# Differential mixer's end: squares ahead of the weight roundings, two gate groups inside the output norm, modulation units one place forward

## What is computed

```python
def diff_attention(...):                      # DA
    def attend(q, k, v):
        s = jnp.einsum('bhmqd,bhmkd->bhmqk', q, k).astype(jnp.float32) * scale
        a = jax.nn.softmax(s, axis=-1)
        a = a[:, :, 0] - lam * a[:, :, 1]
        return jnp.einsum('bhqk,bhkd->bhqd', a.astype(v.dtype), v)
    def finish(o):
        return merge_heads(rmsnorm(o, sub_gain) * (1.0 - lam_init))
...
def hgrn2_mixer(...):                         # HG
    for f, lb in ((f_fw, lower_bound[0]), (f_bw, lower_bound[1])):
        f = lb + (1.0 - lb) * jax.nn.sigmoid(f.astype(jnp.float32))
        dirs.append((split_heads(jnp.log(f), HG_HEADS, HG_DK), split_heads(1.0 - f, HG_HEADS, HG_DK)))
...
for layer in range(DEPTH):
    mod_l = [m[:, None, :] for m in adaln_params(c, w_mod[layer], b_mod[layer])]
    p_l = split_cols(modulate(x, norm1_g[layer], mod_l[0], mod_l[1]) @ w_in[layer])
```

## Time and profile before

| what | value |
|---|---|
| median of three runs | 2334.16 us |
| profiled execution | 2332.5 us |
| its span | 2330.7 us |
| TensorE matmul busy | 2095.5 us (90%) |
| VectorE busy | 999.5 us (43%) |
| ScalarE busy | 784.6 us (34%) |
| GpSimd busy | 697.1 us (30%) |
| mean granted TensorE clock | 0.941 of full speed |

### The profile page before, as it was taken

How to read it: one execution, slowest core, us unless ns; L and a number is a source line. 1 busy time by engine, 2 the same in 40 slices (tenths; PEclk the granted TensorE clock), 3 DMA queues, 4 the chain that set the end, 5 groups by cost and what they waited for, 6 DMA issues and landing times.

```text
span 2330.7 us, 31996 instructions
## 1 busy us (share of the span) xinstructions
PE 2095.5 (90%) x13292; PEld 1752.7 (75%) x13292; DVE 999.5 (43%) x1771; ACT 784.6 (34%) x1281; POOL 697.1 (30%) x573
## 2 busy tenths in 40 slices
PE   5799898878978899999999988998978788999998
PEld 3678786757767788888888866777767667778787
DVE  2545547845674541222213253445847644221222
ACT  1533323423443531222213153223435445232231
POOL 0231211011732323223232222223014433444542
PEclk9899998989988999999999998998989879999999
DMA  8220010451321111212212123010242311322222
GB/s 281 48 71 19 21 35 19 163 140 39 109 73 55 55 55 55 73 55 63 65 55 72 55 45 74 19 37 23 88 109 79 109 55 59 104 91 91 91 91 73
DMA packets 179216, 169.72 MB, mean 73 GB/s; under 512 B 29232, under 2 KB 176128, under 8 KB 178944
## 3 DMA queue, kind: packets, MB, share of 16 engines
q1 hardware_dynamic: 176704, 161.12, 22.6%
q10 hardware_dynamic: 2368, 6.55, 0.9%
HBM read 159.79 MB, written 2.10 MB: 69 GB/s over the span
## 4 chain that ended last, share of the span: by engine, by line
PE 76%; DVE 9%; ACT 7%; issue 3%; DMA 2%; SPq 2%; POOL 1%; DVEq 0%; ACTq 0%; POOLq 0%
PE gp L841 56%; PE sp L1047 3%; PE gp L1084 2%; PE sp L1193 2%; PE tp L1064 1%; SPq L692 1%; PE gp L869 1%; POOL HGx_kd L744 1%; PE sp L1038 1%; DVE small L2073 1%; ACT nt L1372 1%; PE sp L888 1%; PE sp L948 1%; PE op L1064 1%; PE op L1084 1%
## 5 line engine op out<-in xcount | busy, mean ns | idle before, releaser
L756 POOL TENSOR_TENSOR wlo<-raw,whi 128x512 fp32r<-128x512 f32 x392 | 524.6, 1370 | 1348.2 <-ACT whi L1339 1266.8
L841 PE MATMUL gp<-xhi,whi 128*128 128x512 f32 (+1 forms) x1486 | 542.2, 365 | 36.1 <-DVE xlo L1875 21.4
L841 PE MATMUL gp<-xhi,wlo 128*128 128x512 f32 (+1 forms) x1486 | 528.5, 356 | 0.0
L841 PE MATMUL gp<-xlo,whi 128*128 128x512 f32 (+1 forms) x1408 | 502.9, 357 | 0.0
L841 PEld LDWEIGHTS gp<-xhi,whi 128*128 128x128 f32 x1486 | 288.9, 194 | 86.2 <-issue 11.3
L1339 ACT ACTIVATE whi<-raw 128x2048 fp32r<-128x2048 f32 x98 | 186.9, 1908 | 454.2 <-PE gp L841 424.2
L841 PEld LDWEIGHTS gp<-xhi,wlo 128*128 128x128 f32 x1486 | 287.9, 194 | 41.0
L841 PEld LDWEIGHTS gp<-xlo,whi 128*128 128x128 f32 x1408 | 273.7, 194 | 38.6 <-issue 2.0
L841 PE MATMUL gp<-hhi,whi 128*128 128x512 f32 (+1 forms) x768 | 276.5, 360 | 9.6 <-issue 5.0
L841 PE MATMUL gp<-hlo,whi 128*128 128x512 f32 (+1 forms) x768 | 274.9, 358 | 0.0
L841 PE MATMUL gp<-hhi,wlo 128*128 128x512 f32 (+1 forms) x768 | 274.7, 358 | 0.0
(11 more groups left out here) (349 smaller groups left out, 3210.0 us busy)
## 6 DMA issues: line engine op xcount, KB each, us to landing
raw<-in_w_ff SPq DMA_DIRECT2D x64, 1024.0 KB, 5.4
raw<-in_w_mod SPq DMA_DIRECT2D x48, 1024.0 KB, 5.2
raw<-in_w_in SPq DMA_DIRECT2D x20, 1024.0 KB, 5.4
raw<-in_w_in SPq DMA_DIRECT2D x24, 256.0 KB, 4.4
raw<-in_w_out SPq DMA_DIRECT2D x8, 768.0 KB, 4.7
bias<-e SPq DMA_DIRECT2D x96, 32.0 KB
xin<-in_x ACTq DMA_DIRECT2D x1, 2048.0 KB, 9.6
raw<-in_w_out SPq DMA_DIRECT2D x16, 128.0 KB, 4.8
```

Source lines behind the costliest of these rows:

```text
L756: nc.gpsimd.tensor_tensor(wlo[:, s % 2, ks, :], raw[:, index[splits[s]] % 2, ks, :], whi[:, s % 2, ks, :].bitcast(F32), ALU.subtract).then ...
L841: mm = pe.matmul(out, lhs, rhs, start=(i == 0 and j == 0), stop=(i == KT - 1 and j == 2))
```

## The change

Three things change. In `fill_plan` each modulation unit is listed one chunk earlier. TensorE's `out_norm` of DA computes the first two groups of HGf0 itself: the first between the sums and the transposes, the second behind the transposes; `hgrn` then starts HGf0 at its third group. ScalarE stops filling from step 21 on in layer 0 (13 in layer 1), takes the squares, and only then goes through the last five slots, so that both gate roundings stand behind the squares.

```diff
@@ -166,7 +166,7 @@
                 closing = i + 1 < len(chunks) and chunks[i + 1][0] != u
-                while not closing and put < len(units) * (i + 1) // len(chunks):
+                while not closing and put < min(len(units) * (i + 2) // len(chunks), len(units)):
                     work.append((units[put], "row", 3))
...
                 if m == "DA":
-                    out_norm("DA", l, buf("DA", "y"))
-
-            def out_norm(m, l, y):
+                    u = ("prj", l, "HGf0")
+                    out_norm("DA", l, buf("DA", "y"), [lambda i=i: dense(u, chunks_of(u)[i]) for i in range(2)])
+
+            def out_norm(m, l, y, beside=None):
...
                     mm.then_inc(ls(l, m + "_oms"), 1)
+                if beside:
+                    beside[0]()
...
                     mm.then_inc(ls(l, m + "_orstd"), 1)
+                if beside:
+                    beside[1]()
...
                     u = ("prj", l, name)
-                    for c in chunks_of(u):
+                    for c in chunks_of(u)[2 if name == "HGf0" else 0:]:
                         dense(u, c)
...
-                    if n >= 1:
+                    if n >= 1 and (m != "DA" or n <= len(units) - 4):
                         fill(ENDS[m, l][n - 1])
                 if m == "DA":
-                    fill(ENDS[m, l][-2])
-                    fill(ENDS[m, l][-1])
                     end = LAT if l == DEPTH - 1 else T
                     act.wait_ge(*upto(l, "DA_oread", pairs_of("DA", l)))
                     for i in range(2):
                         nc.scalar.activation(buf("DA", "y")[:, i, 0:end], mix[:, i, 0:end], ACT.Square)\
                           .then_inc(ls(l, "DA_osq"), 1)
+                    for slot in ENDS[m, l][-5:]:
+                        fill(slot)
                     out_norm("DA", l, buf("DA", "y"))
```

## The result

The changed kernel takes 2343.01 us, the median of six runs (2340.62 to 2346.88). The kernel before, on the same chip, took 2334.77 (2330.51 to 2336.15, six runs). The ratio is 1.003 with a 95% interval of 1.0016 to 1.0043: the change made the kernel slower by 0.3%. The forecast was 2335 with 2327 to 2342. The measured 2343.01 lies 1.0 above that range; by the ratio, on the 2334.16 that the forecast was worked from, it is 2341.2, just inside. Either way it is 6 to 8 us above the 2335, and of the three cases the slower rival (2342.4) is the one that came.

What follows compares the result with a forecast made beforehand. The prediction took TensorE, with 76% of the chain of waits, to bound the kernel. Terms +5.3 +2.1 +1.75 -5.5 -2.3 = +1.35 on 2332.5 gave 2333.9, plus 1.66 for the median 2335.5, rounded to 2335; range 2327 to 2342.

Steps and rivals of the forecast that it cites:

- the slower rival: Low clock behind most new light steps of DA, four of five in layer 1; sum +8.2, 2342.4 us; chance 0.25.
- the +5.3: Layer 1, steps 6 to 15: chunks moved into odd steps with `weigh`, alternating 4.64 and 6.8; 56.1 against 50.8 us.
- The second sum for the heavy step: Layer 1's heavy odd step checked from step 3: 5.98 plus 0.8 for an eighth of a chunk and a turn, 6.8 us.
- The terms -5.5 and -2.3: End of DA, layers 0 and 1: HGf0 ends at T+33.0 instead of T+38.5, and T+31.0 instead of T+33.3.
- at two in seven and 1.5 us: DA's light steps: two of seven such places bring a low-clock stretch behind them, each costing 1.5 us.
- the clock in the slots: Low-clock cost behind light DA steps, five places in layer 1 and seven in layer 0: +2.1 and +3.0 us.
- the groups of steps of the prediction: Layer 0's DA steps 2 to 23 in four groups at full clock: 38.5, 12.8, 39.5, 15.1, in all 105.9 us.
- the forecast's +1.35: Sum of all terms, DA's steps and ends in both layers, against the profiled 2332.5 us.
- The rival's point of decision (six stretches): Low-clock stretches in DA's steps from which the slower case holds: 3.4 us more than the forecast's 3.4 stretches (5.1 us).
- the norm wins: No low clock in DA's output norm (-8.9 and -5.7) or the new light steps; -7.6, 2326.6 us; chance 0.25.
- the two cancel: The forecast case: the output norm's gain is spent in DA's slots; between 2329.5 and 2338.8 us; chance 0.5.

Runs made afterwards that it cites:

- e9: Kernel before with layer 1's slot 6 left empty and all later contents one slot later, order of work unchanged; 2351.31 us, ratio 1.0058.
- e1: Kernel before with the new plan alone (modulation units listed one chunk earlier); 2336.83 us against 2337.64, ratio 1.0001.
- e2: Changed kernel with the old plan, so only the squares and HGf0 group edits; 2334.42 us, ratio 0.9986 to the kernel before.
- e3: Kernel before with only the squares put ahead of the roundings, no HGf0 groups in the norm; 2327.57 us, ratio 0.9954.
- e6: Changed kernel with HGf0's four groups put back behind the transposes; 2337.59 us, ratio 0.9996 to the kernel before.
- e5: Changed kernel plus ten unread matmuls in DA's light even steps to keep TensorE busy; 2342.12 us, ratio 1.0016 to the kernel before.
- e10: e4 with the new plan line (modulation units one chunk earlier); 2340.28 us, ratio 1.001 to the kernel before.
- e8: e7 plus ten unread matmuls in light even steps; 2324.73 us, ratio 0.994 to the kernel before.
- e4: As e3, with the output norm's factors and spreading also ahead of the deferred roundings; 2323.91 us, ratio 0.9944 to the kernel before.
- e7: As e4, but only the last three slots deferred instead of five; 2322.03 us, ratio 0.9936 to the kernel before.

## Why the prediction was right in the steps and wrong in the clock

**Right: the structure of the steps.** Layer 1 alternates between 4.6 and 6.8 wherever the clock is full, which was the +5.3. With the three low stretches taken off (1.5 each, from 8.32 against 6.79) its 60.78 is 56.2; 56.1 was forecast. (The second sum for the heavy step was loose: an eighth of a chunk and a turn are 0.37 and 0.34, so 6.7 and not 6.8. The first gave 6.85, and 6.79 came.) e9 confirms the reason: it is the exchange between the two kinds of step.

**Right: the end of DA.** Squares at T+0.0, transposes held by HGf0's first group at T+12.6 and T+11.4, TensorE idle for 6.32 and 5.22 before the third group, HGf0's last matmul done at T+33.5 and T+30.9 against T+33.0 and T+31.0 forecast. The terms -5.5 and -2.3 came out as -5.4 and -2.3. The path was right event by event. Where the gain comes from was not: the working gives it to the wait and the roundings that the edit on ScalarE takes away, and allows the plan only one load that comes a step earlier. But the plan's later T alone gives -5.4 and -9.1 (e1), and the other two edits alone -2.9 and -0.7 (e2). The terms hold for the three edits together and for none of them by itself. Nor was the use of the groups questioned: they cost 6 us (e2, e3) to 9 us (changed kernel, e6), and the -5.5 was what was left of a larger gain of the squares.

**Wrong: "at two in seven and 1.5 us".** The term of the sum that failed is the clock in the slots, forecast as +2.1 and +3.0 for 3.4 low stretches of 1.5 us. There were seven: in layer 0 those of steps 7, 12 with 13, 15, and 19, in layer 1 those of steps 9, 13 and 15. In layer 1 they cost 4.6 (60.78 less the 56.1 without them), which is the forecast's price of 1.5 each. In layer 0 the price was wrong too. Each of its slow steps ran at full clock in another kernel with the same plan: 5.49 (e5) instead of 8.59 in step 7, 4.45 and 7.77 (e10) instead of 5.40 and 10.40 in 12 and 13, 6.41 (e10) instead of 7.96 in 15, 4.24 (e5) instead of 6.96 in 19, 3.83 (e1) instead of 4.12 in 20. With these, the groups of steps of the prediction come out as follows:

| steps | forecast, full clock | measured | measured, less the low clock |
|---|---|---|---|
| 2 to 9 | 38.5 | 41.8 | 38.7 |
| 10 to 12 | 12.8 | 13.5 | 12.5 |
| 13 to 19 | 39.5 | 46.0 | 39.1 |
| 20 to 23 | 15.1 | 15.1 | 14.8 |

Together 116.4, and 105.1 without the low clock, against 105.9: the structure of layer 0 was forecast to within 1 us, and four stretches of low clock cost 11.2 us, 2.8 each instead of 1.5. So the low clock cost about 15.8 us in both layers instead of 5.1. These 10.7 us more, less the 0.8 by which layer 0's structure came out shorter, are the way from the forecast's +1.35 to the measured +11.5. The rival's point of decision (six stretches) was passed. That its sum of +8.2 equals the timed +8.2 (2343.01 less 2334.77) is in part luck: it takes eight stretches at 1.5, 12 us of low clock, and the stretches of the trace add up to +11.5. The frequency was taken from seven places of a kernel in which such steps stand alone; the change sets them in a row, each before a heavy step without slack, and there three or four of the five heavy steps 7 to 15 of layer 1 ran at a low clock (e1, e6, e9, e10 and the changed kernel).

For layer 1 the cause is shown, not only argued. With TensorE busy for 4.40 us in the light steps instead of 3.20, all heavy steps behind them run at 1.00 (e5). With the order of the units as before but light and heavy steps alternating, the low clock comes too (e9). Layer 0 fits: the low stretches behind step 2 all began in or behind a step with idle time to which no matmuls had been added, in e5 and e8 as well. This agrees with the Trainium skill, "TensorE: Matmul & The Clock Gate", section "A second HAM failure mode: psum-queue depth-cycling", which tells of a kernel in which short idle times between groups of matmuls make the clock swing and cost throughput: here idle times of 1.4 us in 4.6 suffice, in most places. The prediction had the rule, as a rival at 0.25. Two low stretches out of seven were read as a rate that carries over to any place; it is not a rate.

**The other two rivals.** That the norm wins did not happen: a low clock came in both norms (the sums took 3.80, and the 48 matmuls behind the idle stretch 10.18). That the two cancel is what e1 shows of the plan with the old end, by another way than forecast: not the norm gave it back, but the loads.

**What stays open.**
- What makes the clock fall behind one light step and not behind another. In e9 the steps 1676.98 and 1689.90 are alike but for the last digits (3.19 busy of 4.63, clock 1.00 in both), and 8.29 follows one and 6.79 the other. Where the idle time falls within the step was not varied. Why the low clock lasted two and three times as long in steps 7, 12 with 13, and 19 of layer 0 is open too.
- Why e1 times as before though its stretches of DA are 5.9 longer in sum. Step 5 of layer 1, which lies ahead of the stretches and holds the same work in all kernels, shows how much the clock outside the stretches can shift: 5.34 in before and in the changed kernel, 6.45 to 6.47 in e3, e4, e7 and e9, 7.95 to 7.98 in e1, e2, e6 and e10. The profiled execution of before (2332.5) is 5 us under the median that before had beside e1 (2337.64), and e1's is 2337.44. Low clock elsewhere in other executions of before would explain it; those were not profiled.
- Why e5 turned heavy steps of both layers back to full clock (3.9 and 3.0 us less in the steps) and the total hardly followed: 1.0016 against 1.003, with intervals that overlap. It scatters over 24 us, but so does before in the same job (22.7).

## What to carry to other kernels

Before moving a unit of work from one step of a pipeline to another, write down for each step TensorE's busy time and the length that the other engines give it: work moved out of a step with slack gives nothing back, work moved into a full one is paid whole, and the idle time it leaves may cost the clock of the step behind. Where a phase ends in a wait for a late load, move ahead what does not need the load (here squares and factors), and put no long item between two short ones for which another engine waits. Test each edit alone and again on top of the best version, since a wait that goes away hides the price of whatever lengthened the work before it.

## What the runs showed of the hardware

- In the changed kernel the same 71 matmuls took 8.32 us at a granted clock of 0.79 (step 9 of layer 1) and 6.80 at 1.00 (step 11), with TensorE idle for 1.4 us in the step before either of them. Ten more matmuls of 128 columns in the light step, which cost the step nothing (4.63 in both cases), kept the clock at 1.00 in four of four heavy steps.
- The issuing of eight short transfers on ScalarE's queue stood on the chain that ended last for 5.6 us; in e3, layer 0, it took 6.5, one issue 0.52 to 1.13 us, of which the first four:

```profile
516.67 0.52 ACTq L1586
517.22 0.61 ACTq L1586
517.86 0.78 ACTq L1586
518.67 1.13 ACTq L1586
```

Every version still has them between the norm's final product and the first sigmoid, and none of the runs moved them.
